# State space stage of a fused three-block kernel issued as one stream, with its norms deferred

## The reference, cut to what matters

```python
h = rmsnorm(x, g[0])
z, xBC, dt_raw = split(h @ in_w)                 # 2048, 3072, 32 columns
xBC = silu(causal_dwconv(xBC, conv_w, conv_b))   # width 4
xs, Bm, Cm = split(xBC)                          # 2048, 512, 512
dt = softplus(dt_raw + dt_bias); cs = cumsum(dt * A)      # in a chunk
y_diag = (CB * exp(cs_i - cs_j masked)) @ (xs * dt)
states = Bm^T (decay_to_end * xs * dt)           # chunk 0 feeds chunk 1
y = y_diag + (C @ prev) * exp(cs) + xs * D_skip
y = rmsnorm(y * silu(z), norm_g)
mix = y @ out_w
x = x + rmsnorm(mix, g[1])
```

## Time and profile before

| | |
|---|---|
| median of 3 runs | 3445.69 us (3440.66 to 3445.71) |
| the profiled execution's own time | 3439.73 us |
| its span on the core | 3437.9 us |
| mean granted TensorE clock | 0.982 of full |
| state space stage, from the start to the first `ssm_out` matmul | 261.7 us |
| of it the recurrence, C times B to the last output | 72.8 us |

### The profile page before, as it was taken

One profiled execution on the slowest core, in us unless ns is written; L12 is line 12 of the kernel. 1 busy time (PEld: TensorE's weight loads), 2 busy tenths in 40 slices (PEclk: granted clock), 3 DMA queues, 4 the chain that ended last, 5 costly groups with the idle time before them and its releaser, 6 DMA issues.

```text
span 3437.9 us, 39895 instructions
## 1 busy us (share of the span) xinstructions
PE 3284.9 (96%) x15934; PEld 2487.7 (72%) x15934; DVE 863.1 (25%) x1894; ACT 623.4 (18%) x1150; POOL 232.4 (7%) x195
## 2 busy tenths in 40 slices
PE   8969999999999989999999999999799999999997
PEld 7857888888888867888778888788544444444444
DVE  2153132166332144101321024441211111111111
ACT  2121111211221025100220013340111111111111
POOL 0020010000010010100211011210000000000000
PEclk9989999999999999999999999999899999999999
DMA  5403334432234431444324344224499999999996
GB/s 211 155 18 123 112 133 156 163 135 86 98 136 156 156 115 63 183 158 147 112 104 164 133 157 169 77 98 149 187 412 422 422 422 422 422 422 422 422 422 256
DMA packets 98437, 714.92 MB, mean 208 GB/s; under 512 B 10992, under 2 KB 10992, under 8 KB 11664
## 3 DMA queue, kind: packets, MB, share of 16 engines
q1 hardware_dynamic: 97632, 710.07, 52.8%
q0 software_dynamic: 688, 3.15, 0.3%
HBM read 712.12 MB, written 1.05 MB: 207 GB/s over the span
## 4 chain that ended last, share of the span: by engine, by line
PE 79%; DMA 14%; DVE 5%; ACT 1%; issue 1%; SPq 0%; POOL 0%; DVEq 0%; ACTq 0%; POOLq 0%
PE bank L272 48%; DMA weight_ring<-in_stream 14%; PE bank L291 8%; PE bank L2800 7%; PE bank L2832 3%; PE bank L2772 1%; PE bank L2764 1%; PE bank L2136 1%; PE bank L401 1%; DVE residual L998 1%; PE bank L1329 1%; PE bank L797 1%; PE bank L470 0%; DVE arena L996 0%; PE bank L327 0%
## 5 line engine op out<-in xcount | busy, mean ns | idle before, releaser
L272 PE MATMUL bank<-normed_residual,weight_ring 128*128 128x256 f32 x4256 | 931.9, 380 | 0.0
L272 PEld LDWEIGHTS bank<-normed_residual,weight_ring 128*128 128x128 f32 x4256 | 808.0, 190 | 115.7 <-issue 7.1
L272 PE MATMUL bank<-arena,weight_ring 128*128 128x256 f32 x2920 | 639.8, 381 | 8.1 <-ACT arena L1381 3.9
L272 PEld LDWEIGHTS bank<-arena,weight_ring 128*128 128x128 f32 x2920 | 558.2, 191 | 86.4 <-issue 8.5
L2800 PE MATMUL bank<-weight_ring,arena 128*64 128x512 f32 x2048 | 449.1, 593 | 15.2 <-DMA weight_ring<-in_stream 14.2
L2800 PEld LDWEIGHTS bank<-weight_ring,arena 128*64 128x64 f32 x2048 | 150.1, 137 | 308.3 <-issue 308.2
L2832 PE MATMUL bank<-arena 128*64 128x512 f32 x1024 | 226.8, 595 | 0.0
L291 PE MATMUL bank<-gained_residual,weight_ring 128*128 128x256 f32 x832 | 191.9, 391 | 7.5 <-DVE gained_residual L361 7.5
L291 PEld LDWEIGHTS bank<-gained_residual,weight_ring 128*128 128x128 f32 x832 | 164.0, 198 | 33.1 <-DVE gained_residual L361 9.1
L2892 DVE TENSOR_TENSOR arena<-bank,arena 128x512 f32<-128x512 f32 x32 | 22.1, 692 | 634.3 <-PE bank L2800 634.3
L2832 PEld LDWEIGHTS bank<-arena 128*64 128x64 f32 x1024 | 70.7, 137 | 131.8 <-issue 127.9
(11 more groups left out here) (361 smaller groups left out, 2497.0 us busy)
## 6 DMA issues: line engine op xcount, KB each, us to landing
weight_ring<-in_stream SPq DMA_DIRECT2D x546, 1024.0 KB, 6.4
arena<-in_stream SPq DMA_DIRECT2D x128, 1024.0 KB, 16.7
residual<-in_x SPq DMA_DIRECT2D x1, 1024.0 KB, 4.8
arena<-in_mem POOLq DMA_DIRECT2D x1, 1024.0 KB, 5.1
out<-arena SPq DMA_DIRECT2D x1, 1024.0 KB, 3.9
constants<-in_con SPq DMA_DIRECT2D x1, 608.5 KB, 7.1
vectors<-in_vec SPq DMA_DIRECT2D x1, 548.5 KB, 6.1
arena<-in_p POOLq DMA_DIRECT2D x2, 256.0 KB, 3.0
```

Of the source, the lines that this page charges most:

```text
L272: mm = nc.tensor.matmul(PB[b][:, m * T:m * T + T], l, r, start=(kc == 0), stop=(kc == chunks - 1))
```

## The change

- The order of the x pairs becomes 8 to 11 (B and C), then 0 to 7. The stage starts with a sweep over pairs 8 and 9 instead of a norm, with the statistics after the fifth tile.
- The x and z pairs use two PSUM banks in turn instead of four. The other banks serve the recurrence.
- After pairs 10 and 11, 32 halves (8 x pairs, 8 z pairs) are issued as slots 0 to 31, and the parts of the recurrence follow fixed slots: C times B after half 1, transposes after 5, 13, 18, 22, broadcasts after the slots in `CR_AT`, outputs two slots behind. Odd batches' outputs share bank 6 with the state matmul. ScalarE and VectorE go through the same slots. Both `meet` are gone.
- The gate product of two tiles comes on VectorE in slots 18 to 32. ScalarE squares it and writes it with the gain into Z. `ssm_out` reads Z un-normed; POOL sums the squares, PE takes the statistics after the second half, and the root is folded into the variance of the result (one more VectorE instruction) and into its reciprocal (another).
- The sweeps of `ff_in0`, `ff_in1`, `b1_1_in`, `xa_in1` and `b2_0_in` take their statistics after the fifth tile, not the third.
- The `lam` products, the small matmul and its Exp move from the start of the second block to the end of `ffn_in1`.

```diff
-ORDER = whole("ssm_x", "ssm_z", "ssm_out", "xa_k0")
+SSM_X = (8, 9, 10, 11, 0, 1, 2, 3, 4, 5, 6, 7)
+ORDER = [("ssm_x", _p) for _p in SSM_X] + whole("ssm_z", "ssm_out", "xa_k0")
...
+NARROW = ("ssm_x", "ssm_z", "lat", "hq", "uqn", "uqr", "uk", "uv", "hi", "hg", "ga", "gb", "brb", "bra")
...
+        CR_AT = (6, 8, 10, 12, 14, 16, 17, 18, 19, 20, 21, 22, 23, 24, 25, 26)
+        Y_AT = tuple(s + 2 for s in CR_AT)
+        XT_AT = (5, 13, 18, 22)
+        CB_AT = 1
+        Z_AT = 16
+        GATE_AT = (18, 20, 22, 24, 26, 28, 30, 32)
...
+        def x_source(k):
+            p = SSM_X[k]
+            return A[:, SWEPT0 + 2 * k:SWEPT0 + 2 * k + 2, :] if k < 2 else bank(bank_of("ssm_x", p))
...
+        def ssm_slot_pe(pe, s):
+            if s == CB_AT:
+                pe.wait_ge(sem["xbc_ready"], 4)
+                pe.wait_ge(sem["pre_std"], 1)
+                for c in range(2):
+                    for g in range(4):
+                        mm = nc.tensor.matmul(PB[6 + c][:, g * P:g * P + P], A[:, XBC + 16 + g, c * P:c * P + P],
+                                              A[:, XBC + 20 + g, c * P:c * P + P], start=True, stop=True)
+                    mm.then_inc(sem["cb_mm"], 1)
+                for g in range(4):
+                    mm = nc.tensor.transpose(PB[2][:, g * P:g * P + P], A[:, XBC + 16 + g, 0:P], ident)
+                mm.then_inc(sem["cb_mm"], 1)
+            if s in XT_AT:
+                g = XT_AT.index(s)
+                pe.wait_ge(sem["xbc_ready"], 4 + 2 * g + 2)
+                if g:
+                    pe.wait_ge(sem["xdt_ready"], 2 * g)
+                else:
+                    pe.wait_ge(sem["btok_ready"], 1)
+                for cc in range(2):
+                    for k in range(4):
+                        mm = nc.tensor.transpose(PB[2 + cc][:, k * P:k * P + P],
+                                                 A[:, XBC + 4 * g + k, cc * P:cc * P + P], ident)
+                    mm.then_inc(sem["xt_mm"], 1)
+            if s in CR_AT:
+                i = CR_AT.index(s)
+                g, half, c = batch(i)
+                pe.wait_ge(sem["dte_in"], 1)
+                if i >= 2:
+                    pe.wait_ge(sem["seg_ready"], i - 1)
+                if i >= 3:
+                    pe.wait_ge(sem["ecs_ready"], (i - 1) // 2)
+                for k in range(4):
+                    h = g * HPG + half * 4 + k
+                    mm = nc.tensor.matmul(PB[4 + i % 2][:, k * P:k * P + P], DTA[:, c, h:h + 1].broadcast_to([P, P]),
+                                          upto, start=True, stop=True)
+                mm.then_inc(sem["cr_mm"], 1)
+                if i % 4 == 0:
+                    pe.wait_ge(sem["btok_ready"], 1)
+                    pe.wait_ge(sem["xde_ready"], g + 1)
+                    pe.wait_ge(sem["cbm_ready"], 2)
+                    if g:
+                        pe.wait_ge(sem["y_ready"], 4 * g - 2)
+                    nc.tensor.matmul(PB[6][:, :], flat(BTOK, 2)[:, g * P:g * P + P], flat(XDE, 2), start=True,
+                                     stop=True).then_inc(sem["st_mm"], 1)
+            if s in Y_AT:
+                j = Y_AT.index(s)
+                g, half, c = batch(j)
+                pe.wait_ge(sem["g_ready"], j + 1)
+                if j >= 2:
+                    pe.wait_ge(sem["y_ready"], j - 1)
+                pe.wait_ge(sem["st_ready"], before(CR_AT[0:16:4], s + 1))
+                if c:
+                    pe.wait_ge(sem["cp_ready"], j // 2 + 1)
+                for k in range(4):
+                    o = y_bank(j)[64 * (k % 2):64 * (k % 2) + 64, k // 2 * P:k // 2 * P + P]
+                    hs = slice((half * 4 + k) * 64, (half * 4 + k) * 64 + 64)
+                    mm = nc.tensor.matmul(o, xdt(g, c)[:, hs], flat(GW + 2 * (j % 2), 2)[:, k * P:k * P + P],
+                                          start=True, stop=(c == 0))
+                    if c:
+                        mm = nc.tensor.matmul(o, flat(STATE + 2 * (g % 2), 2)[:, hs],
+                                              flat(CEX + 2 * (half % 2), 2)[:, k * P:k * P + P], start=False, stop=True)
+                mm.then_inc(sem["y_mm"], 1)
+        def ssm_pe(pe):
             pe.wait_ge(sem["vec_in"], 32)
-            norm_pe(pe, "b1_0_in")
-            pe.wait_ge(sem["normed"], 8)
+            sweep_pe(pe, "b1_0_in", [("ssm_x", 8), ("ssm_x", 9)], 4)
...
+            for p in (10, 11):
+                for m in range(2):
+                    half_pe(pe, "ssm_x", p, m, ht)
...
+            for s in range(32):
+                half_pe(pe, "ssm_x" if s < Z_AT else "ssm_z", s % Z_AT // 2, s % 2, ht)
+                ssm_slot_pe(pe, s)
...
+        def ssm_slot_act(act, s):
...
+            if s < Z_AT and s % 2:
+                base_act(act, 4 + s // 2)
+            if s < Z_AT + 1 and s and s % 2 == 0:
+                silu_act(act, 3 + s // 2)
+            if s >= Z_AT and s % 2 and s < 32:
+                copy_pair_act(act, "ssm_z", (s - Z_AT) // 2, A[:, Z + s - Z_AT - 1:Z + s - Z_AT + 1, :], ACT.Silu)
+            if s in GATE_AT:
+                q = GATE_AT.index(s)
+                act.wait_ge(sem["gated"], q + 1)
+                nc.scalar.activation(A[:, SQ2 + 2 * q:SQ2 + 2 * q + 2, :], A[:, XBC + 2 * q:XBC + 2 * q + 2, :],
+                                     ACT.Square).then_inc(sem["sq_pair"], 1)
+                for j in range(2):
+                    t = 2 * q + j
+                    ins = nc.scalar.activation(A[:, Z + t, :], A[:, XBC + t, :], ACT.Identity, scale=vec("ssm_ng", t))
+                ins.then_inc(sem["gate_gain"], 1)
...
+            if s in GATE_AT:
+                q = GATE_AT.index(s)
+                wait_evac(dve, "ssm_z", q)
+                dve.wait_ge(sem["y_ready"], 8 * (q // 2) // 2 + 4)
+                y, z = (A[:, b + 2 * q:b + 2 * q + 2, :] for b in (XBC, Z))
+                nc.vector.tensor_tensor(y, y, z, ALU.mult).then_inc(sem["gated"], 1)
...
-            norm_pe(pe, "ssm")
             for p in range(4):
                 for m in range(2):
-                    half_pe(pe, "ssm_out", p, m, yt, ready=normed_ready("ssm") if p == 0 else None)
-                    if p == 0 and m == 0:
+                    half_pe(pe, "ssm_out", p, m, tiles(Z),
+                            ready=(lambda e, kc: e.wait_ge(sem["gate_gain"], kc // 2 + 1)) if p == 0 else None)
+                    if p == 0 and m == 1:
+                        pe.wait_ge(sem["sq_sum"], SUMS["gate"] + 1)
+                        for t in range(2):
+                            mm = nc.tensor.matmul(PB[6][:, 0:T], ones, A[:, SQ2 + t, :], start=(t == 0), stop=(t == 1))
+                        mm.then_inc(sem["pre_stat"], 1)
+                    if p == 1 and m == 0:
                         norm_pe(pe, "mem")
...
+            dve.wait_ge(sem["pre_stat"], PRE["b1_0_mix"] + 1)
+            nc.vector.tensor_tensor(MIXVAR, STAT, SSMR2, ALU.mult).then_inc(sem["second_in"], 1)
+            post_dve(dve, own, "b1_0_mix", "ssm_out", "xa_in0", g1(0, 2), SSMR)
...
-                sweep_pe(pe, "xa_in1", [("xa_q1", 0), ("xa_q1", 1)], 2)
+                sweep_pe(pe, "xa_in1", [("xa_q1", 0), ("xa_q1", 1)], 4)
...
-            sweep_pe(pe, f"ff_in{l}", [(name, 0), (name, 1)], 2)
+            sweep_pe(pe, f"ff_in{l}", [(name, 0), (name, 1)], 4)
             for p in range(2, 22):
                 for m in range(2):
                     half_pe(pe, name, p, m, ht, ready=h_after(f"ff_in{l}") if p == 2 else None)
+            if l:
+                pe.wait_ge(sem["lam_in"], 1)
+                nc.tensor.matmul(PB[6][:, 0:8], ones, LAMP, start=True, stop=True).then_inc(sem["lam_mm"], 1)
...
             if l == 1:
+                for k in range(2):
+                    ins = nc.vector.tensor_tensor(LAMP[:, 4 * k:4 * k + 4], vec("lam", 8 * k, 4), vec("lam", 8 * k + 4, 4),
+                                                  ALU.mult)
+                ins.then_inc(sem["lam_in"], 1)
                 tables_dve(dve, own, "pos2", vec("inv2", 0))
+                dve.wait_ge(sem["lam_exp"], 1)
+                own(nc.vector.tensor_tensor(LAM, LAME[:, 0:4], LAME[:, 4:8], ALU.subtract))
+                own.wait()
+                own(nc.vector.tensor_scalar(LAM, LAM, LAM_INIT, None, ALU.add))
+                nc.vector.tensor_scalar(SUBG, vec("subln", 0), 1.0 - LAM_INIT, None, ALU.mult).then_inc(sem["lam_ready"], 1)
             post_gain_dve(dve, f"ff_out{l}", f"ffn_out{l}", g1(l, 5))
...
-            sweep_pe(pe, "b1_1_in", [("pw1", 0), ("pw1", 1)], 2)
+            sweep_pe(pe, "b1_1_in", [("pw1", 0), ("pw1", 1)], 4)
...
         def even_pe(pe):
-            pe.wait_ge(sem["lam_in"], 1)
-            nc.tensor.matmul(PB[6][:, 0:8], ones, LAMP, start=True, stop=True).then_inc(sem["lam_mm"], 1)
-            sweep_pe(pe, "b2_0_in", EVEN[0:2], 2)
+            sweep_pe(pe, "b2_0_in", EVEN[0:2], 4)
```

417 lines of the change are left out of this document (197 added, 220 removed).

## The result

| | before | changed |
|---|---|---|
| median | 3445.70 us (3440.66 to 3452.39, 4 runs) | **3363.44 us** (3361.73 to 3363.57, 4 runs) |
| profiled execution, its span | 3437.9 us | 3359.9 us |
| granted clock, mean | 0.982 | 0.99 |
| first `ssm_out` matmul | 261.73 us | 203.08 us |

The ratio of changed to before is 0.9762, with a 95% interval of 0.9745 to 0.9779. The forecast was 3363 in a range of 3347 to 3394. The medians lie 82.3 us apart, the two profiled executions 78.0 in span: the profiled execution of the kernel before took 3439.73 us, less than any of its four runs.

The account below looks back on a forecast made before the run. PE was taken as the bound, with time to gain only where it waits or runs at half clock. -59.8 + 0.0 - 17.1 - 2.5 = -79.4 from 3439.7 gives 3360.3, plus 3: 3363 us, range 3347 to 3394.

Parts of the forecast that it names:

- The opening: First sweep starts when the second weight unit lands at 13.9 us and ends at 30.4; dt matmuls end at 33.9.
- The recurrence's own work: PE's transposes, broadcasts, state matmuls and outputs of the recurrence within the stream: 37.9 us.
- The three waits: At slots 14, 19 and 23 an output waits for ScalarE's state copy in a shared bank: 1.8 us each, 5.4 in all.
- Behind the stream: At `ssm_out` and the next norm, 1.8 us of half clock goes, two matmuls and two VectorE instructions come: net 0.0.
- The sweeps: Statistics after the fifth tile shorten PE's waits for POOL's sum: gain 3 x 5.2 + 1.5 = 17.1 us.
- `lam`: Matmul moved to the end of `ffn_in1`: 8.4 us gained, 5.9 lost to a new wait and half clock, net gain 2.5.
- a longer expert stage: Sign of being wrong: the expert stage, which the change leaves untouched, takes longer; no size given.
- the last step from 3360.3 to 3363: 3 us added to the sum, since three shown runs lie 0.9 to 6.0 us above the profiled execution.
- Table loads: Rival: each of 24 ScalarE table loads in slots 6 to 28 delays PE, 31 us: 3394; chance 0.08.
- Clock: Rival: the mixed stream runs at clock 0.89 from slot 0 on, 19 us longer: 3382; chance 0.10.
- Sweeps: Rival: sum or normed input comes later with the tiles, PE waits as before, 17 us missing: 3380; chance 0.05.
- Two banks: Rival: x and z pairs from slot 6 wait for their PSUM bank, 7.7 us each, 100 in all: 3463; chance 0.02.

Follow-up runs that it names:

- State copy ahead: Changed kernel with group 1's state matmul one slot later and each state copy last in its slot on ScalarE: 3356.55 us, ratio 0.9750.
- changed again: The changed kernel itself, unedited, rerun on the same chip and beside the same runs as three edited kernels: 3363.08 us, ratio 0.9768.
- the run with the old place: Changed kernel with the lam products, matmul and Exp back at the start of block 2's first mixer: 3365.11 us, ratio 0.9777.
- all three: Changed kernel with state copies last in their slots, constants loaded behind two weight units, lam products ahead of the convs: 3351.10 us, ratio 0.9734.
- sweeps back: Changed kernel with the statistics of the five sweeps back at the third tile: 3382.04 us, ratio 0.9824.
- the Identity kernel: Changed kernel with Identity for the Silu of the x and z linears, so no table switches in slots 6 to 28: 3362.90 us, ratio 0.9771.
- both sweep kernels: Changed kernel with five sweeps' statistics back at the third tile, 3382.04 us; kernel before with them at the fifth, 3426.19 us.
- the kernel with one round of loads: Changed kernel with an extra one-column Silu and Exp on ScalarE in even slots 16 to 26, 10 more table loads: 3368.42 us, ratio 0.9787.
- the one-slot kernel: Changed kernel with each output asked for one slot after its broadcast instead of two: 3380.67 us, ratio 0.9822.
- the two kernels with the constants third: Changed kernel with constants loaded behind the first two weight units, alone 3363.44 us; also with state copies last and lam products ahead of convs, 3351.10 us.

## Why the prediction was right

- **The opening.** The second unit was to land at 13.9 and the sweep to end at 30.4: 14.10 and 29.47. I had charged 2.7 us of half clock; the 36 records from 14.10 on took 9.3 us to the statistics, where 7.8 is full pace, so 1.6. (The column of the granted clock reads 1.00 from 14 us on; it is the pace, 4 records a us up to 17 and 6 to 7 from there, that shows the slow start.) The dt matmuls took 3.5, as taken.
- **The recurrence's own work** was the term that was short: 37.9 forecast, about 40.2 found (155.6 less 5.0 of waits and 32 halves of 3.45). This is the largest miss of the sum. The rows name it. Between the outputs and a half, start to start, the half takes 3.56 (142.39 to 145.95) and the broadcasts in front of an output 0.98 (145.95 to 146.93), where broadcasts before a half take 0.90 and a half after them 3.45 (127.45, 128.35, 131.80). That is 0.1 us for each change between weights of 128 and of 64 columns, 3.1 us for 16 batches with two each. Against it, my 0.93 for eight records was too long: transposes between halves took 0.87 (131.80 to 132.68) and broadcasts 0.90, 1.0 less over the 24 sets. The 0.93 was read at 187.88 in the earlier trace rows, behind outputs of 64 columns, so it held such a change already. The width is my reading of the rows; no run varies it by itself.
- **The three waits** at the group starts: 1.8 each forecast, 1.79, 1.60 and 1.60 found. State copy ahead shows that the copy is the cause. The prediction's reason, a shared bank, holds for the first only; the other two waits came from the semaphore count, as shown above. The first `ssm_out` matmul came at 203.1, forecast 201.9.
- **Behind the stream** +1.0 instead of 0.0. The wait for POOL's sum was 4.22, where the 3.27 of the earlier trace rows and the two new instructions make 4.2. What the sum lacked stands behind this wait: the 68 records from the statistics on took 17.64 us before (341.10 to 358.74) and 16.47 in the changed kernel, 1.2 less:

```profile
282.57 1.38 PE L333 MATMUL bank<-arena,constants 128*128 128x256 f32 x4 [4.22 <-POOL arena L324]
283.75 15.45 PE L274 MATMUL bank<-arena,weight_ring 128*128 128x256 f32 x64
299.04 13.98 PE L274 MATMUL bank<-normed_residual,weight_ring 128*128 128x256 f32 x64
```

  In *changed again* they took 17.55 (283.74 to 301.29), and 16.2 to 17.6 in the variants, all behind a wait of 4.2. So I read this 1.0 as the moment when the clock rises, not as a gain of the change.
- **The sweeps**: 17.1 forecast, 18.7 found. `b1_1_in` gave 6.0, and `ff_in1` 2.5 instead of 1.5. The normed input was in time.
- **`lam`**: 2.5 forecast, 2.1 found; the wait 3.07 instead of 3.4, the clock 2.7 instead of 2.0. By the run with the old place only 1.0 of it is left when the other parts of the change are in.
- **Not in the sum**: 2.5 us given back at the end of the lead table, 1.6 of them in the first expert matmuls, eight of 512 columns. Before, then changed:

```profile
2456.93 5.09 PE L2779 MATMUL bank<-arena 128*128 128x512 f32 x8 [2.52 <-DVE arena L2880]
```

```profile
2376.43 6.71 PE L2887 MATMUL bank<-arena 128*128 128x512 f32 x8 [2.53 <-DVE arena L2988]
```

Same work, same wait, 1.6 us longer, since the clock rose later: it was granted at 0.50 up to 2382.4 in the changed kernel, 6.0 us into the row, and at 0.81 already from 2459 to 2461 before, 2 to 4 us into it. In the runs these eight took 5.2 (all three, sweeps back), 6.3, 6.5, 6.6 and 6.7 (changed again); in the kernel before with the sweeps at the fifth tile 6.3. The moment when the clock rises varies from execution to execution with and without the change; what sets it is open. The prediction had named a longer expert stage as a sign of being wrong. By this row it did take longer, but *all three*, which holds the whole change, has 5.18 there, so the sign does not speak against the mechanism. The other 0.9 lies at the very end, of which 0.7 in the 16 statistics matmuls of the last norm, which took 6.25 us instead of 5.52.

The errors had both signs and came to 1.4 us in the gain of the profiled pair (79.4 against 78.0): that they cancel so far is luck. So is the last step from 3360.3 to 3363, 3 us added for the spread of the kernel before; the changed kernel's median lies 1.7 above its profiled execution, and the other 1.4 are the sum's error. The rivals all fell. Table loads: by the Identity kernel. Clock: 1.00 in the stream of the profiled execution. Sweeps: by both sweep kernels. Two banks: no wait of a half for its bank in the list. That the mixed stream does not hold the clock was nearer than the result shows: the waits of 2.84 us in the kernel with one round of loads did pull it down, and so did one of 1.78 us in *changed again*.

## What to carry to other kernels

Work that waits for round trips between engines is covered best by independent matmuls of the same stage, and the distance is the thing to choose: list the chain (here 3.7 us by the prediction's count) and everything queued ahead of each of its links, and put the consumer behind more than that. After such a change look at the waits that remain for ones that only share a buffer or a counter with what is waited for, and at small operands that are made at the end of a queue though their inputs were there long before: two such edits gave 5.2 and 5.8 us here by the rows. Price a wait of PE as its length, plus the half clock behind it where the clock falls, here 1.1 to 2.9 us for waits of 1.8 to 3.1.

## What the runs showed of the chip

- **When the clock falls.** PE's waits of 1.60 us at the group starts never brought it down (14 in seven executions). The wait of 1.78 did in three of nine. In the one-slot kernel one of the eight of 1.82 did, and the one of 2.02. The two of 2.84 both did, and so did the 3.07 before `lam`, in all nine executions that have it. The price, read from a half or a pair behind it, is 1.1 to 1.7 us for the shorter ones (4.83, 5.17 and 5.41 against 3.72, 8.86 against 7.17) and 1.7 to 2.9 for that of 3.07 (308 records in 68.41 to 69.56 us, against 66.64 to 66.72 in the three executions without the wait).
- **The opening has two forms.** Where the first 36 records of the sweep took 8.6 to 8.9 us (three executions), the two pairs after dt took 15.75; where the 36 took 9.2 to 10.1 (seven), the pairs took 14.06 (the two kernels with the constants third, which wait once in between, apart). State copy ahead, in PE's timeline:

```profile
13.98 8.88 PE L293 MATMUL bank<-gained_residual,weight_ring 128*128 128x256 f32 x36 [0.36 <-DMA weight_ring<-in_stream]
...
32.24 15.75 PE L274 MATMUL bank<-normed_residual,weight_ring 128*128 128x256 f32 x64
```

  The granted clock of this execution is 0.70 from 32 to 34 us and 0.50 from 34 to 36, where the changed kernel has 1.00. PE does not stand in between; it does the dt matmuls, of 32 columns each. No run tests what makes the clock fall there.
- **Weights of another width.** By the rows above, a change between weight tiles of 128 and 64 columns costs PE about 0.1 us each way (a half 3.56 instead of 3.45, broadcasts 0.98 instead of 0.90); no run tests it alone. The Trainium skill, "TensorEngine Tiling (Array Packing)", section "Key Properties", says that a change of tiling mode drains TensorE, without a figure; the rows fit that.
- **VectorE beside GpSimd.** VectorE's gate product of 128x512 took 0.69 us at best and 1.50 in the middle of its eight; in the case looked at it started at 149.20 while POOL's product ran from 148.88 to 150.15. The one of 0.69, at 203.91, had no product of POOL beside it. The one in the middle ended at 150.70, 0.55 behind POOL's end. No run takes POOL's away.
